# The mLSTM gates of a two-layer hybrid block: kept in rows, one direction per group of 32 partitions, and summed by scans

## What is computed

```python
def _mlstm_features(p, conv_w, conv_b, gate_b):
    q, k, v, o, i_f, i_b, f_f, f_b = _split(p, MLSTM_COLS)
    ...
    dirs = ((qh, kh, vh, i_f + gate_b[0], jax.nn.log_sigmoid((f_f + gate_b[2]).astype(jnp.float32))),
            (qh, kh, vh, i_b + gate_b[1], jax.nn.log_sigmoid((f_b + gate_b[3]).astype(jnp.float32))))
...
        b = jnp.cumsum(fc, axis=-1)
        log_w = jnp.where(causal, b[..., :, None] - b[..., None, :] + ic[..., None, :], MASK_NEG)
        m_t = jnp.maximum(log_inter, jnp.max(log_w, axis=-1))
        w = jnp.exp(log_w - m_t[..., None]) * jnp.einsum('bhtd,bhsd->bhts', qc, kc)
        floor = jnp.exp(jnp.minimum(-m_t, MAX_NEG_LOG_STAB))
```

## Time and profile before

| | |
|---|---|
| time, median of 3 runs | 1713.68 us (1712.07 to 1714.19) |
| the profiled execution, its own time | 1715.59 us |
| its span, first to last instruction | 1713.8 us |
| PE busy | 1583.7 us, 92% of the span |
| PEld, DVE, ACT, POOL busy | 1253.4, 1059.7, 645.5, 70.0 us |
| mean granted clock of PE | 0.952 |
| this stage in layer 0 | from about 163 us of the span, its broadcasts from 204.8 us |
| this stage in layer 1 | from about 1117 us, its broadcasts from 1151.8 us |

### The profile page before, as it was taken

How to read it: one execution, slowest core, us unless ns; L and a number is a source line. 1 busy time by engine, 2 the same in 40 slices (tenths; PEclk the granted TensorE clock), 3 DMA queues, 4 the chain that set the end, 5 groups by cost and what they waited for, 6 DMA issues and landing times. The chain is left out here.

```text
span 1713.8 us, 28786 instructions
## 1 busy us (share of the span) xinstructions
PE 1583.7 (92%) x11804; PEld 1253.4 (73%) x11804; DVE 1059.7 (62%) x1812; ACT 645.5 (38%) x1100; POOL 70.0 (4%) x110
## 2 busy tenths in 40 slices
PE   6999999969899999999999979999978898999997
PEld 4766776745688688888888867778754677678885
DVE  2286345897867574554443365734776866578766
ACT  4355222445321263222222253433245321366652
POOL 0000011300100000000000000000010110000000
PEclk8999899989999999999999989999979899899998
DMA  9411111166101143222232032222236101355561
GB/s 389 149 61 38 54 58 49 38 230 240 52 3 52 50 190 130 99 98 99 93 105 74 0 115 74 62 61 75 74 127 244 52 2 52 111 190 190 197 202 44
DMA packets 41330, 180.93 MB, mean 106 GB/s; under 512 B 4720, under 2 KB 5488, under 8 KB 33392
## 3 DMA queue, kind: packets, MB, share of 16 engines
q1 hardware_dynamic: 41200, 179.09, 29.7%
HBM read 178.03 MB, written 1.05 MB: 104 GB/s over the span
## 5 line engine op out<-in xcount | busy, mean ns | idle before, releaser
L236 PE MATMUL ps<-hr_in,wr_in 128*128 128x512 f32 (+1 forms) x544 | 221.9, 408 | 12.4 <-DVE wr_in L229 11.5
L238 PE MATMUL ps<-hr_in,wr_in 128*128 128x512 f32 (+1 forms) x544 | 210.0, 386 | 0.0
L237 PE MATMUL ps<-hr_in,wr_in 128*128 128x512 f32 (+1 forms) x544 | 210.0, 386 | 0.0
L236 PEld LDWEIGHTS ps<-hr_in,wr_in 128*128 128x128 f32 x544 | 109.5, 201 | 62.5 <-issue 36.0
L229 DVE TENSOR_TENSOR wr_in<-mix,wr_in 128x1024 fp32r<-128x1024 f32 x68 | 83.9, 1234 | 88.2 <-ACT wr_in L225 84.8
L236 PE MATMUL ps<-mix_r,work_r 128*128 128x512 f32 (+1 forms) x352 | 133.8, 380 | 1.6 <-DVE work_r L229 1.6
L237 PE MATMUL ps<-work_r 128*128 128x512 f32 (+1 forms) x356 | 135.1, 379 | 0.0
L229 DVE TENSOR_TENSOR work_r<-pr,work_r 128x2048 fp32r<-128x2048 f32 x38 | 86.9, 2288 | 67.7 <-ACT work_r L225 63.6
L238 PE MATMUL ps<-mix_r,work_r 128*128 128x512 f32 x320 | 124.5, 389 | 0.0
L238 PEld LDWEIGHTS ps<-hr_in,wr_in 128*128 128x128 f32 x544 | 109.2, 201 | 19.5
L237 PEld LDWEIGHTS ps<-hr_in,wr_in 128*128 128x128 f32 x544 | 109.5, 201 | 15.6 <-issue 0.2
(11 more groups left out here) (536 smaller groups left out, 3258.5 us busy)
## 6 DMA issues: line engine op xcount, KB each, us to landing
mix<-in_w_in SPq DMA_DIRECT2D x68, 512.0 KB, 3.6
pr<-in_w_up SPq DMA_DIRECT2D x28, 1024.0 KB, 4.9
pr<-in_ada_w SPq DMA_DIRECT2D x40, 512.0 KB, 6.8
ring<-in_w_up SPq DMA_DIRECT2D x16, 1024.0 KB, 4.9
ring<-in_ada_w SPq DMA_DIRECT2D x28, 512.0 KB, 4.5
pr<-in_w_down SPq DMA_DIRECT2D x14, 1024.0 KB, 5.0
pr<-in_ada_w SPq DMA_DIRECT2D x8, 1024.0 KB, 15.8
work<-in_w_out SPq DMA_DIRECT2D x16, 512.0 KB, 3.7
```

The costliest lines, as they stand in the source:

```text
L236: nc.tensor.matmul(out, sh, mh, start=first, stop=False)
L237: nc.tensor.matmul(out, sh, ml, start=False, stop=False)
L238: return nc.tensor.matmul(out, sl, mh, start=False, stop=last)
```

## The change

The input weights are laid out anew, so that the projection delivers the gates as rows of tile `T_GD2`: partitions 64 to 67 hold f of direction 0 for the 4 heads and 68 to 71 its i, 96 to 99 and 100 to 103 the same of direction 1. `both` takes 36 partitions with both directions in one instruction. Bias, log sigmoid, sums, `net`, maxima and levels are made on these rows, 512 tokens along the free axis; one DMA within SBUF moves the i rows down by 4 partitions onto the f rows. The running sums are scans with a constant 1 as factor. The triangular products, the turning of the gates and ACT's copies are gone. PE turns `net` to tokens (`by_tokens`, 8 matmuls) after all but two of the WAIT turns, and later the levels in the place of `tops`. The broadcasts take their 4 rows from two row groups of the array (`tile_position` 64 and 96), one per direction. ACT does the HEAD turns ahead of the table load.

```diff
-GATE_ROW = 32
+GATE_AT = 64
...
-    brow = ws[1][0:4, 0:1024]
+    biased, lf, i_rows = (ws[1][:, n * T:(n + 1) * T] for n in range(3))
+    before, net = biased, tops[:, T:2 * T]
...
+    def gate_rows(t, d, a=0, b=T):
+
+return t[GATE_AT + 32 * d:GATE_AT + 32 * d + 4, a:b]
+
+    def both(t, n=36, first=GATE_AT):
+return t[first:first + n, 0:T]
+
     def top(d, a=0, b=T):
-return tops[0:4, d * T + a:d * T + b]
+return gate_rows(tops, d, a, b)
...
     sp.dma_start(condw[:, 0:2 * KD], E["A"]["cond"]).then_inc(S("cond"), 16)
+    sp.wait_ge(S("biased"), 1)
+    sp.dma_start(both(i_rows), both(biased, first=GATE_AT + 4)).then_inc(S("i_rows"), 16)
     for t in range(proj.first + 2, min(proj.end + 2, proj.n)):
...
-    for j in range(TILES):
-        mm = nc.tensor.transpose(ps[0][:, j * 64:(j + 1) * 64], pr[0:64, T_GD2 * T + j * P:T_GD2 * T + (j + 1) * P], c(C_ID, 64, 64))
-    mm.then_inc(S("gates"), 1)
...
-    for i in range(HEAD):
+
+    def by_tokens(src, o):
+        for j in range(TILES):
+            for d in range(2):
+                r = GATE_AT + 32 * d
+                mm = nc.tensor.matmul(ps[6 - 2 * d][:, o + j * 4:o + j * 4 + 4], gate_rows(src, d, j * P, (j + 1) * P),
+                                      const[r:r + 4, C_ID + r:C_ID + r + 4], start=True, stop=True, tile_position=(r, 0))
+        return mm
+
+    for i in range(L0 - 2):
         proj.pe_turn(pe, i)
-    pe.wait_ge(S("lf"), 1)
+    pe.wait_ge(S("net"), 1)
+    by_tokens(net, 288).then_inc(S("netT"), 1)
+    for i in range(L0 - 2, L0):
+        proj.pe_turn(pe, i)
     pe.wait_ge(S("vT_out"), 1)
-    for d in range(2):
-        for j in range(TILES):
-            out = ps[1 + d][0:4, j * P:(j + 1) * P]
-            for n, s in enumerate((*earlier(d, j), j)):
-                nc.tensor.matmul(out, lf[:, s * 8 + d * 4:s * 8 + d * 4 + 4], c(C_ONES) if s != j else c(C_TRI + d * P),
-                                 start=(n == 0), stop=(s == j))
-        for j in range(TILES):
-            nc.tensor.matmul(ps[3 + d][0:4, j * P:(j + 1) * P], gt[:, j, d * 4:d * 4 + 4], ident, start=True, stop=True)
-    for d in range(2):
-        for j in range(TILES):
-            out = ps[6][:, 288 + j * 8 + d * 4:288 + j * 8 + d * 4 + 4]
-            for n, s in enumerate((*earlier(d, j), j)):
-                mm = nc.tensor.matmul(out, c(C_ONES) if s != j else c(C_TRI + d * P), lf[:, s * 8 + d * 4:s * 8 + d * 4 + 4],
-                                      start=(n == 0), stop=(s == j))
-    mm.then_inc(S("rows"), 1)
-    for i in range(HEAD, L0):
-        proj.pe_turn(pe, i)
...
         for d in range(2):
-            mm = nc.tensor.matmul(ps[d][:, lo0:], c(C_SELH + hd * P, P, 4), top(d, lo0), start=True, stop=True)
+            r = GATE_AT + 32 * d
+            mm = nc.tensor.matmul(ps[d][:, lo0:], const[r:r + 4, C_SELH + hd * P:C_SELH + (hd + 1) * P], top(d, lo0),
+                                  start=True, stop=True, tile_position=(r, 0))
...
         if hd == 0:
-            pe.wait_ge(S("brow_used"), 1)
-            for d in range(2):
-                for j in range(TILES):
-                    mm = nc.tensor.matmul(ps[6][:, 256 + j * 8 + d * 4:256 + j * 8 + d * 4 + 4], top(d, j * P, (j + 1) * P), c(C_ID, 4, 4),
-                                          start=True, stop=True)
-            mm.then_inc(S("topT"), 1)
+            pe.wait_ge(S("levels"), 1)
+            pe.wait_ge(S("gc"), 1)
+            by_tokens(i_rows, 256).then_inc(S("levelT"), 1)
...
-    dve.wait_ge(S("gates"), 1)
-    gb = par[:, Q_GB:Q_GB + 16].rearrange("p (j g) -> p j g", j=1).to_broadcast([P, TILES, 16])
-    g4 = small[:, 0:64].rearrange("p (j g) -> p j g", j=TILES)
-    link(nc.vector.tensor_tensor(g4, ps[0][:, 0:256].rearrange("p (j g) -> p j g", j=TILES)[:, :, GATE_ROW:GATE_ROW + 16], gb, ALU.add))
-    f = g4[:, :, 8:16]
-    lf3, la3, lb3 = (v.rearrange("p (j g) -> p j g", j=TILES) for v in (lf, la, lb_))
-
-    link(nc.vector.tensor_scalar(la3, f, -1.0, None, ALU.mult))
-    link(nc.vector.tensor_tensor(la3, la3, f, ALU.min))
-    nc.vector.tensor_scalar(lb3, f, 0.0, None, ALU.min).then_inc(S("absf"), 1)
+    nc.vector.tensor_scalar(both(biased, 40), both(tiles(pr, T_GD2, 1), 40), par[GATE_AT:GATE_AT + 40, Q_GB:Q_GB + 1], None, ALU.add)\
+        .then_inc(S("biased"), 1)
+    dve.wait_ge(S("biased"), 1)
+    nc.vector.scalar_tensor_tensor(out=both(lf), in0=both(biased), scalar=-1.0, in1=both(biased), op0=ALU.mult, op1=ALU.min)\
+        .then_inc(S("absf"), 1)
...
     for i in range(HEAD):
         proj.dve_turn(dve, i)
     dve.wait_ge(S("lnf"), 1)
-    nc.vector.tensor_tensor(lf3, lb3, la3, ALU.subtract).then_inc(S("lf"), 1)
-    dve.wait_ge(S("brow"), 1)
-    nc.vector.tensor_tensor(gc.rearrange("p (j g) -> p j g", j=TILES), g4[:, :, 0:8],
-                            ps[6][:, 288:320].rearrange("p (j g) -> p j g", j=TILES), ALU.subtract)
+    link(nc.vector.scalar_tensor_tensor(out=both(lf), in0=both(biased), scalar=0.0, in1=both(lf), op0=ALU.min, op1=ALU.subtract))
+    for i in range(HEAD, HEAD + 2):
+        proj.dve_turn(dve, i)
+
+    def along(out, src, d, op0, op1):
+
+        def first(v, n):
+            r = GATE_AT + 32 * d
+            return const[r:r + 4, C_ONES:C_ONES + 1].to_broadcast([4, n]) if op0 == ALU.mult else v
+
+        if d == 0:
+            v = gate_rows(src, 0)
+            return nc.vector.tensor_tensor_scan(gate_rows(out, 0), first(v, T), v, 0.0, op0, op1)
+        v, w = (forward(gate_rows(src, 1, a, a + SIDE), 1) for a in (0, SIDE))
+        link(nc.vector.tensor_tensor_scan(forward(gate_rows(out, 1, 0, SIDE), 1), first(v, SIDE), v, 0.0, op0, op1))
+        return nc.vector.tensor_tensor_scan(forward(gate_rows(out, 1, SIDE, T), 1), first(w, SIDE), w, gate_rows(out, 1, 0, 1), op0, op1)
+
+    dve.wait_ge(S("i_rows"), 16)
+    along(before, lf, 0, ALU.mult, ALU.add)
+    link(along(before, lf, 1, ALU.mult, ALU.add))
+    nc.vector.tensor_tensor(both(net), both(i_rows), both(before), ALU.subtract).then_inc(S("net"), 1)
+    dve.wait_ge(S("net"), 1)
+    along(tops, net, 0, ALU.max, ALU.max)
+    along(tops, net, 1, ALU.max, ALU.max).then_inc(S("maxed"), 1)
+    dve.wait_ge(S("maxed"), 1)
     for d in range(2):
-        ins = nc.vector.tensor_tensor(top(d), ps[3 + d][0:4, :], brow[:, d * T:(d + 1) * T], ALU.subtract)
-    ins.then_inc(S("brow_used"), 1)
-    dve.wait_ge(S("brow_used"), 1)
-    nc.vector.tensor_tensor_scan(top(0), top(0), top(0), 0.0, ALU.max, ALU.max)
-    ctx_b, lat_b = (forward(top(1, a, a + SIDE), 1) for a in (0, SIDE))
-    link(nc.vector.tensor_tensor_scan(ctx_b, ctx_b, ctx_b, 0.0, ALU.max, ALU.max))
-    nc.vector.tensor_tensor_scan(lat_b, lat_b, lat_b, top(1, 0, 1), ALU.max, ALU.max).then_inc(S("maxed"), 1)
-    for i in range(HEAD, L0):
+        ins = nc.vector.tensor_tensor(gate_rows(i_rows, d), gate_rows(before, d), top(d), ALU.add)
+    ins.then_inc(S("levels"), 1)
+    for i in range(HEAD + 2, L0):
         proj.dve_turn(dve, i)
...
-        t3 = ps[6][:, 256:288].rearrange("p (j d h) -> p h d j", j=TILES, d=2)
-        b3 = ps[6][:, 288:320].rearrange("p (j d h) -> p h d j", j=TILES, d=2)
-        dve.wait_ge(S("topT"), 1)
-        for hd in range(HEADS):
-            ins = nc.vector.tensor_copy(f3[:, hd], b3[:, hd])
-        link(ins)
-        for hd in range(HEADS):
-            ins = nc.vector.tensor_tensor(f3[:, hd], f3[:, hd], t3[:, hd], ALU.add)
+        dve.wait_ge(S("levelT"), 1)
+        for d in range(2):
+            ins = nc.vector.tensor_copy(f3[:, :, d, :], ps[6 - 2 * d][:, 256:272].rearrange("p (j h) -> p h j", j=TILES))
...
+    dve.wait_ge(S("netT"), 1)
+    for d in range(2):
+        ins = nc.vector.tensor_copy(gc.rearrange("p (j d h) -> p j d h", j=TILES, d=2)[:, :, d, :],
+                                    ps[6 - 2 * d][:, 288:304].rearrange("p (j h) -> p j h", j=TILES))
+    ins.then_inc(S("gc"), 1)
+    dve.wait_ge(S("gc"), 1)
...
     ins.then_inc(S("vT_out"), 1)
+    for i in range(HEAD):
+        proj.act_turn(act, i)
     nc.scalar.preload_act_table_set(LN_EXP)
     act.wait_ge(S("absf"), 1)
-    nc.scalar.activation(la, la, ACT.Exp).then_inc(S("link_act"), 1)
+    nc.scalar.activation(both(lf), both(lf), ACT.Exp).then_inc(S("link_act"), 1)
     if layer:
         act.wait_ge(S("lb_in"), 1)
         nc.scalar.activation(col[:, 6:10], col[:, 6:10], ACT.Exp).then_inc(S("lb_exp"), 1)
     act.wait_ge(S("link_act"), 1)
-    nc.scalar.activation(la, la, ACT.Ln, bias=1.0).then_inc(S("lnf"), 1)
-    for i in range(HEAD):
-        proj.act_turn(act, i)
-    act.wait_ge(S("rows"), 1)
-    nc.scalar.copy(brow[:, 0:T], ps[1][0:4, :])
-    nc.scalar.copy(brow[:, T:2 * T], ps[2][0:4, :]).then_inc(S("brow"), 1)
+    nc.scalar.activation(both(lf), both(lf), ACT.Ln, bias=1.0).then_inc(S("lnf"), 1)
     for i in range(HEAD, L0):
         proj.act_turn(act, i)
```

More of the change, by code:

```diff
@@ L979, in mlstm @@
     nj = len(js)
+    const = E["const"]
     lo0, _ = span(layer)
@@ L1007, in mlstm @@
```

(21 more changed lines are left out.)

1 line of the change is left out of this document (removed).

## The result

The changed kernel takes **1667.86 us** (median of 4 runs, 1661.98 to 1673.93) against 1712.88 for the kernel before on the same chip: ratio 0.9749, 95% interval 0.9715 to 0.9782. Two later measurements of the same kernel gave 0.9786 [0.9762, 0.9809] and 0.9765 [0.9732, 0.9797]. Scaled to the 1713.68 of before, the three say 1670.7, 1677.0 and 1673.4. The forecast was 1681.6 with a low end of 1674: the direction is right, the gain larger than forecast, by 4.6 to 10.9 us over the three (13.7 from the forecast to the first median as it stands).

The account below looks back on a forecast made before the run. PE was taken to bound the stage; 13.9 us (layer 0) plus 13.1 (layer 1) ahead of the broadcasts and 5.1 in them made 32.1 off, giving 1681.6 us from the median of 1713.68, range 1674 to 1688.

Parts of the forecast that it names:

- The bound: PE bounds the rest of the stage; every PE-microsecond saved ahead of or in the broadcasts moves what follows.
- chain B, C, D on ACT and DVE: Weights of projection tiles, layer 0: low parts ready at about 170.8, 174.9 and 183.2; PE waits for B and D, not C.
- B's wait: PE's idle ahead of projection tile B in layer 0, waiting for its weights: 0.8 us.
- three signs of being wrong: PE waits over 4 us ahead of D; clock falls longer than behind L1150; savings return as waits for `normed` or weights.
- The old by-token group of the same size, L1150, takes 1.94; I take 1.9: New 8-matmul group turning `net` to tokens, ahead of the broadcasts: 1.9 us, with a clock fall behind it losing 1.6.
- The by-token groups also overlap by row group: Rival: four groups of 1.94 us at half, old clock falls gone too; about 1671 us, chance 0.06.
- I take the broadcasts' start as the measure of each layer: First broadcasts start at 190.8 for 204.78 in layer 0 and 1138.7 for 1151.80 in layer 1.
- the 5.1 us of the pairs: Broadcast pairs from two row groups take 1.13 and 0.70 us for 1.98 and 1.12: 3.4 saved in layer 0, 1.7 in layer 1.
- the forecast had 27.0: Time saved ahead of the first broadcasts: 13.9 us in layer 0 and 13.1 in layer 1.
- No fall behind the `net` groups: Forecast took a clock fall there, 1.6 us a layer; the rival without it gave 1678.4 us, chance 0.22.
- Waits ahead of D: PE's idle ahead of projection tile D, waiting for its weights: 1.5 us in layer 0, none in layer 1.
- DVE's chain ahead of D: Six scans, `net` and two level sums on DVE ahead of tile D's low part: 7.05 us.

Follow-up runs that it names:

- The kernel with few products: The kernel before with 18 of the 20 by-token products of a layer left out: 1695.73 us, 0.9909.
- the third execution: The changed kernel unedited, measured a third time: 1670.18 us, 0.9765 of the kernel before.
- the two near-copies of before: The kernel before, once with L1150's matmuls given tile position (0, 0), once with L1150's second direction in another bank: 1714.87 and 1717.88 us.

## Why the prediction was partly right

**Right.** The bound: what PE saved ahead of the broadcasts arrived at the stage's end and did not come back as waits (the waits of the earlier trace rows grew from 2.0 to 3.5 us in layer 0). The products and the wait ahead of them gone; chain B, C, D on ACT and DVE, with B's wait 0.88 for 0.8; broadcast pairs 1.13 and 0.70 to the hundredth; scans 1.22, 0.69, 0.75; activations on rows 0.63 for 0.57. The kernel with few products shows the clock's part. Of the prediction's three signs of being wrong, one showed, and only in the third execution: a fall of 6.8 us at the `net` group, longer than the 3.4 behind L1150.

**The steps that failed** are two, both on PE's small matmuls.

The first is "The old by-token group of the same size, L1150, takes 1.94; I take 1.9", with the fall of the clock taken behind it. The groups took 1.06, and in two executions of three no fall stood at the `net` groups. The rival that had this, "The by-token groups also overlap by row group", got a chance of 0.06 and a time of 1671, on the argument that with 4 columns the matmuls cost 0.12 each whatever their form. But neither row behind that argument had two row groups, so they could not bear on the question, and the second of them, L1092 at 2.35/20, is no 4-column matmul: it streams 128 columns. The row that did bear on it, the scores of the earlier trace rows, spoke for overlap, and I let it speak for the broadcasts alone. 16 instructions in 1.06 are 0.066 each. The Trainium skill's rule, which I set beside it ("TensorEngine Tiling (Array Packing)", Instruction Overhead), is not to take a tiling factor from a dimension that is already small. Here the factor is taken from the rows, and it is the columns, 4 of them, that are few. My reading, that few columns leave nothing to gain, is contradicted by these runs.

The second is a term put at nothing: "I take the broadcasts' start as the measure of each layer", with only the 5.1 us of the pairs behind it. Ahead of the broadcasts the trace gives 15.35 + 13.91 = 29.3 us where the forecast had 27.0. Behind their start it gives 13.2 where the forecast had 5.1. So 8.1 of the 10.4 us missed lie there, in the falls of the clock behind the later small matmuls and in the second by-token group.

**The bill**, trace against forecast, 42.5 against 32.1:
- Four by-token groups, 0.88 each: 3.5 more.
- No fall behind the `net` groups, 1.6 a layer: 3.2 more. In the third run layer 0 had one after all, and lost 3.1 by it.
- Waits ahead of D, 2.05 and 1.04 for 1.5 and 0: 1.6 less. DVE's chain ahead of D took 7.64 for 7.05, hand-overs that I had left out; and in layer 1 the shorter group brought PE to D 0.9 earlier than forecast, so most of that wait is this gain waited away (with groups of 1.52 it was 0.57).
- Falls behind the start of the first broadcasts, 27.3 us low before and 6.8 after, both layers. At half speed this is 10.2 at most. Of it the forecast had nothing. Later waits for weights took some back: 1.6 in layer 0 (2.08 for 0.49 at the fourth head) and 0.9 in layer 1.
- These make 12.8, where 10.4 are to be explained. The 10.2 is an upper bound, since PE did not work through all of that time.

**What decides how much falls** is not settled. Broadcasts from one row group, with the directions one after the other in the groups, gave five falls ahead of layer 0's last values; the changed kernel gave none or one. But the same kernel fell at D's wait in one execution of three, and the two near-copies of before had three and four falls in layer 0 for its five. Over the fifteen profiles, the falls between a stage's start and its last values count 6 in the 14 stages whose small matmuls all alternate between row groups, 16 in the 8 with one or both of these undone, and 28 in the 8 of before, its two near-copies and the kernel with few products. So falls are rarer with the overlap; which place will fall is not predicted by anything here, and no run separates the shorter groups from whatever else decides it.

**Also open:** why, with the directions one after the other, the first pair comes with the fifth start and not sooner; the group lies so halfway between 1.06 and 1.94.

**The range.** It ended at 1674 because the chance of 0.06 was left out. The two effects of that rival and the falls of the later heads go the same way, so they should have stood as one case with much more chance.

## What to carry to other kernels

Small serial sums in rows belong on DVE's scans while PE has blocks that do not need them, but the next weights must stand ahead of them in DVE's order: that place was worth 2.3 and 1.3 us here. Small matmuls from alternating row groups took 0.55 to 0.63 of the time of those from one, down to 4 columns. Count each stretch of small matmuls twice, once for its length and once for the clock behind it, and look at every such stretch of the stage, not only at those that the change edits.

## What was not expected of the hardware

- 4-column float32 matmuls overlap between two row groups: 16 instructions in 1.06 us alternating, 1.52 one direction after the other, 1.94 from one row group, with one bank or two. Instructions of one row group start 0.11 us apart in all of these; those of the other run beside them.
- The change of row groups has no price that shows: the broadcasts of layer 0 start 0.32 after the start of the matmul ahead of them (190.22 behind 189.90), as they did before, and the `qk` behind them starts 0.07 ahead of the pair's recorded end in both kernels.
- The clock's falls are not a property of the program alone: the same instructions fell at 184.3 for 6.8 us in one execution and not in two others.
